# Where the two halves of a recurrence level stand on TensorE's queue, beside the attention blocks

## The chip, the cores and the metric

The kernel runs on one core of one Trainium2 chip. The metric is the device time of one execution in microseconds (us); of several runs the median is taken. In the rows, PE is TensorE, PEld its weight loads, DVE VectorE, ACT ScalarE, POOL GpSimd and SP SyncE.

## What is computed

One inference step of two hybrid decoder layers, for a prompt of 16 + 512 tokens and eight sample tokens. Each layer projects its input once and runs two mixers on the result: a sparse attention, in which an indexer picks the keys of each query, and a gated linear recurrence (HGRN2). Their outputs are gated, merged and projected, and a SwiGLU feed-forward follows. Of the recurrence the prompt's part matters here, computed in its exact chunk form:

```python
b = jnp.cumsum(logf.astype(jnp.float32), axis=1)
diff = b[:, :, None] - b[:, None, :]
decay = jnp.exp(jnp.where(causal[None, :, :, None, None], diff, -jnp.inf))
scores = jnp.einsum('bthk,bshk,btshk->bths', q, k, decay)
o = jnp.einsum('bths,bshv->bthv', scores, v) + jnp.einsum('bthk,bhkv->bthv', q * jnp.exp(b), S0)
```

and of the attention the softmax over the picked keys and its product with the values:

```python
s = jnp.where(valid[:, :, None, None, :], s, -jnp.inf)
p = jax.nn.softmax(s, axis=-1)
o = jnp.einsum('btngk,btknd->btngd', p, v_sel.astype(jnp.float32))
```

## The kernel before, in words

Each engine has its own instruction list, written out by hand; the lists meet only through semaphores. An engine works its list strictly in order, so a wait at its head holds up all that stands behind it. Most of a layer is one long run of weight units: 512 KB of weights are loaded, split by ACT and POOL into a high and a low part, and multiplied by PE in fp32. Between the input projection and the merge lies a stretch without weight units. In it 17 attention blocks (`BLK`, line 153; a block is one pair of heads by one tile of up to 128 queries) and the recurrence of the prompt are interleaved, over 20 steps of one loop (`STEPS`, line 144). The change lies in this stretch.

**An attention block** goes round three engines. PE multiplies queries and keys into `acc` (`qk`, line 1126, products at line 1143). DVE adds the mask and takes the row maximum (`att_scores`, line 2515, instruction at line 2528). ACT takes the exponential (`att_exps`, line 1739, at 1745), DVE the reciprocal of the sums (`att_recips`, line 2532, at 2536), ACT scales to probabilities (`att_probs`, line 1748, at 1754). PE turns the probabilities (`turn`, line 1147; transposes carry line 800), ACT copies them back to SBUF (`att_turned`, line 1756, at 1763), PE multiplies them with the values (`pv`, line 1162, products at line 1175) and ACT drains the result (`att_drain`, line 1646, at 1658). PE forms the query-key products two blocks ahead.

**The recurrence** splits the causal scores of a chunk of 128 tokens into a diagonal and seven levels, with blocks of 64, 32, 16, 8, 4, 2 and 1 tokens. For each level DVE forms differences of the summed log decays (`level_diff`), ACT takes their exponentials (`level_exp`, at line 1673), and DVE multiplies them with queries and keys (`level_product`, lines 2445 and 2447). PE multiplies the outcome with itself, for two heads at a time: the two halves of a level (`level`, line 1221, at 1227; eight fp32 products, which the trace shows as 16 records). DVE copies what the level's mask lets through into the score table `Asc` (`level_scores`, line 2411, at 2417). Four of the levels have a small product for the last 16 tokens besides (`level_tail`, line 1231, at 1238). Both halves of all levels use one PSUM tile, the whole of `work[1]`, and `rec_begin` (line 1181) makes a half wait until DVE has copied the half before:

```python
if n >= 1 and (rec_full(n) or rec_full(n - 1)):
    wait_rec_drained(pe, L, rec[n - 1])
```

**The order.** PE's loop works a block as: the steps of `PE_AHEAD`, the query-key products of the block after next, the turn of this block, the steps of `PE_AMID`, the value product of this block, the steps of `PE_BEHIND` (lines 1320 to 1335). DVE's loop (line 2540) works: the scores of the next block, `DVE_AHEAD`, the reciprocal of the next block, `DVE_BEHIND`; the copy of a level's first half is the last step of `DVE_BEHIND` in the level's block, that of the second half stands in `DVE_AHEAD` of the next block. ACT's loop (line 1773) works: probabilities, drain of the block before, exponentials of the next block, `ACT_AHEAD`, the turned probabilities, `ACT_BEHIND`. SP starts the load of the recurrence's sample states once the last level and tail are formed (line 614).

Of the kernel before, what the change touches and what calls it, by code (L numbers as in the profile page):

```python
# [76 lines left out]
def build(nc, t, out):  # L77
# [69 lines left out]
    for c in range(5):  # L147
# [3 lines left out]
    REC_ODD = [(RECS + 1) // 2, RECS // 2]  # L151
    TAILS = [7, 3, 4, 5, 6]
    BLK = [(0, 0), (0, 1), (0, 2), (0, 4), (0, 3)] + [(n2, j) for n2 in range(1, 4) for j in range(4)]
    PE_AHEAD = {1: [("diagonal", 0)], 2: [("diagonal", 1)], 4: [("level", 0, 0)], 6: [("level", 1, 0)],
                7: [("level", 2, 0)], 9: [("level", 3, 0), ("level_tail", 3)], 10: [("level", 4, 0), ("level_tail", 4)],
                12: [("level", 5, 0), ("level_tail", 5)], 13: [("level", 6, 0), ("level_tail", 6)]}
    PE_AMID = {3: [("v_turn", 3), ("v_turn", 4)], 4: [("level", 0, 1)],
               6: [("level", 1, 1)], 7: [("level", 2, 1)], 9: [("level", 3, 1)], 10: [("level", 4, 1)],
               12: [("level", 5, 1)], 13: [("level", 6, 1)], 14: [("decayed", 0)], 15: [("decayed", 1)],
               16: [("decayed", 2)], 17: [("decayed", 3)], 18: [("decayed", 4)]}  # L160
    PE_BEHIND = {3: [("level_tail", 7)], 14: [("rec_out", 0), ("state", 0), ("rank1", 0)], 15: [("rec_out", 1), ("state", 1), ("rank1", 1)],
                 16: [("rec_out", 2), ("state", 2), ("rank1", 2)], 17: [("rec_out", 3), ("state", 3)],
# [35 lines left out]
    with ctx:  # L198
# [62 lines left out]
        def place(name, shape, offset, dt=f32):  # L261

            n = 1
            for d in shape[1:]:
                n *= d
            n *= 1 if dt == u8 else 4
            assert offset + n <= size, (name, offset + n, size)
            return nc.alloc_sbuf_tensor_at(name, shape, dt, offset=base + offset)
# [56 lines left out]
        decayed = place("decayed", [P, 2, 512], 6 * TB + 5 * 2048)  # L325
# [469 lines left out]
        def _(pe):  # L795
# [18 lines left out]
            for L in range(DEPTH):  # L814
# [332 lines left out]
                def turn(block, s):  # L1147

                    n2, j = BLK[block]
                    ps = turn_tile_of(s)  # L1150
                    if L * BLOCKS + block:
                        pe.wait_ge(turn_drained[s], L * BLOCKS + block)
                        wait(pe, "pv_drained", L, BLOCKS, block)
                    wait(pe, "probs", L, 2 * BLOCKS, 2 * block + s + 1)
                    hold(pe)
                    for c in range(j + 1):
                        w = min(P, WIDTH[j] - c * P)
                        at = ps[0:w, c * P:c * P + P] if c < 4 else last_turn(s)
                        mm = transpose(at, scores_of(block, s, c * P, c * P + w))
                    mm.then_inc(turn_filled[s], 1)  # L1160
# [146 lines left out]
                def rec_steps(steps):  # L1307

                    for step in steps:
                        if isinstance(step, tuple):  # L1310
                            rec_step[step[0]](*step[1:])
                        else:
                            sample_turn(step)
# [6 lines left out]
                for block in range(STEPS):  # L1320
                    rec_steps(PE_AHEAD.get(block, ()))
                    if block + 2 < BLOCKS:
# [6 lines left out]
                    if block < BLOCKS:  # L1329
                        turn(block, 0)  # L1330
                        turn(block, 1)
                    rec_steps(PE_AMID.get(block, ()))
                    if block < BLOCKS:
# [1370 lines left out]
```

## Time and profile before

| | us |
|---|---|
| median of 3 runs | 2100.64 |
| lowest and highest | 2096.79, 2101.87 |
| the profiled execution | 2106.03 |
| its span, first to last instruction | 2104.1 |
| PE busy in the span | 1990.2 |

The profile is of one execution. Its page gives, per engine, the busy time, the chain of work that ended last, and the costliest groups of instructions; the trace behind it gives each instruction's start, length and, in brackets, how long its engine stood idle before it and what ended that.
### The profile page before, as it was taken

The numbers are of one execution on the slowest core, as the hardware profiler recorded it, in microseconds if no ns is written. First come the engines' busy times: TensorE is split into PE (matmuls) and PEld (weight loads), VectorE is DVE, ScalarE is ACT, GpSimd is POOL, SyncE is SP. The second block draws the span as 40 slices with busy tenths as digits, with TensorE's granted clock in tenths as the row PEclk, the third lists the DMA queues.
The fourth block names the chain that finished last, engine by engine and source line by source line (L and its number), as shares of the span: only waits on it lengthen the run. The fifth ranks groups of instructions, "written<-read, shape, count | busy, mean of one in ns | idle before, by whom it ended". The sixth has DMA issues, their size and how long they took to land.

```text
span 2104.1 us, 40077 instructions
## 1 busy us (share of the span) xinstructions
PE 1990.2 (95%) x15610; PEld 1889.6 (90%) x15610; DVE 1179.8 (56%) x2150; ACT 774.6 (37%) x1207; POOL 761.8 (36%) x418
## 2 busy tenths in 40 slices
PE   6999999888989999999999899998889999999998
PEld 6988899866889999999998889997678999999998
DVE  4477788676466442055346677986764664412531
ACT  4334222476234333222423342235652343322222
POOL 2633347200044434444455223661002444334342
PEclk9999999898899999999999999998998999999999
DMA  6332235202332332322241322442033323233322
GB/s 157 93 91 61 71 112 172 90 2 73 95 113 80 90 90 75 103 85 75 85 148 53 91 61 75 138 143 70 1 103 107 111 81 89 80 89 101 89 67 85
DMA packets 310126, 189.18 MB, mean 90 GB/s; under 512 B 15992, under 2 KB 295768, under 8 KB 308976
## 3 DMA queue, kind: packets, MB, share of 16 engines
q1 hardware_dynamic: 300368, 160.51, 26.9%
q0 software_dynamic: 4224, 16.78, 2.4%
q10 hardware_dynamic: 5408, 10.16, 1.4%
q8 instruction: 85, 1.39, 0.3%
q14 instruction: 41, 0.34, 0.1%
HBM read 167.47 MB, written 18.10 MB: 88 GB/s over the span
## 4 chain that ended last, share of the span: by engine, by line
PE 80%; DVE 7%; issue 5%; ACT 4%; POOL 3%; DMA 1%; POOLq 0%; SPq 0%; DVEq 0%; ACTq 0%
PE acc L839 64%; PE work L1227 3%; PE work L800 2%; POOL w_lo L685 2%; PE work L1175 1%; PE work L978 1%; POOL k_sel L751 1%; DVE std L1953 1%; PE acc L1143 1%; PE work L1262 1%; PE work L1081 1%; PE work L865 1%; PE work L1043 1%; DVE mix L2602 1%; ACT w_hi L1435 1%
## 5 line engine op out<-in xcount | busy, mean ns | idle before, releaser
L685 POOL TENSOR_TENSOR w_lo<-raw,w_hi 128x1024 fp32r<-128x1024 f32 (+3 forms) x290 | 623.8, 2152 | 1225.8 <-ACT w_hi L1435 1221.2
L839 PE MATMUL acc<-normed,w_hi 128*128 128x268 f32 x5696 | 958.5, 290 | 4.3 <-POOL w_lo L685 2.9
L839 PEld LDWEIGHTS acc<-normed,w_hi 128*128 128x128 f32 x5696 | 802.0, 190 | 27.3 <-issue 20.1
L1435 ACT ACTIVATE w_hi<-raw 128x1024 fp32r<-128x1024 f32 (+1 forms) x286 | 289.0, 1011 | 936.0 <-PE acc L839 936.0
L839 PE MATMUL acc<-normed,w_lo 128*128 128x268 f32 x2848 | 585.6, 287 | 0.0
L839 PEld LDWEIGHTS acc<-normed,w_lo 128*128 128x128 f32 x2848 | 446.3, 189 | 0.0
L839 PE MATMUL acc<-hidden,w_hi 128*128 128x268 f32 x1408 | 231.4, 286 | 0.0
L839 PEld LDWEIGHTS acc<-hidden,w_hi 128*128 128x128 f32 x1408 | 196.9, 188 | 0.0
L839 PE MATMUL acc<-hidden,w_lo 128*128 128x268 f32 x704 | 144.1, 286 | 0.0
L2639 DVE TENSOR_TENSOR hidden<-act_f,hidden 128x536 f32 x44 | 92.8, 2110 | 51.1 <-ACT hidden L1853 51.1
L2632 DVE TENSOR_TENSOR silu<-silu,rnorm 128x536 f32<-128x536 f32 x44 | 83.4, 1895 | 59.1 <-ACT silu L1850 59.1
L839 PEld LDWEIGHTS acc<-hidden,w_lo 128*128 128x128 f32 x704 | 109.7, 188 | 0.0
L2614 DVE TENSOR_TENSOR x<-acc,x 128x536 f32<-128x536 f32 x32 | 22.9, 717 | 127.5 <-PE acc L839 127.5
L839 PE MATMUL acc<-merged,w_hi 128*128 128x268 f32 x512 | 84.6, 287 | 4.8 <-issue 3.2
L2649 DVE TENSOR_TENSOR x<-acc,x 128x536 f32 x16 | 11.5, 716 | 125.6 <-PE acc L839 125.6
L2629 DVE TENSOR_TENSOR silu<-acc,rnorm 128x536 f32<-128x536 f32 x44 | 31.5, 717 | 84.7 <-PE acc L839 84.0
L1227 PE MATMUL work<-X 128*128 128x128 f32 x448 | 63.6, 301 | 16.2 <-issue 14.6
L1227 PEld LDWEIGHTS work<-X 128*128 128x128 f32 x448 | 59.1, 213 | 21.0 <-issue 20.9
L839 PEld LDWEIGHTS acc<-merged,w_hi 128*128 128x128 f32 x512 | 71.7, 188 | 5.6 <-issue 5.6
L2635 DVE TENSOR_TENSOR act_f<-acc,silu 128x536 f32<-128x536 f32 x44 | 31.5, 716 | 80.2 <-PE acc L839 80.0
L1467 ACT ACTIVATE relu<-work 128x256 f32<-128x256 f32 (+4 forms) x66 | 31.6, 503 | 85.9 <-PE work L978 68.1
L1929 DVE TENSOR_TENSOR proj_att<-acc,rnorm 128x536 f32<-128x536 f32 x26 | 18.4, 712 | 64.8 <-PE acc L839 59.0
(345 smaller groups left out, 2801.2 us busy)
## 6 DMA issues: line engine op xcount, KB each, us to landing
raw<-in_w_in_dram SPq DMA_DIRECT2D x90, 512.0 KB, 3.8
raw<-in_w_gu_dram SPq DMA_DIRECT2D x88, 512.0 KB, 3.8
raw<-in_w_down_dram SPq DMA_DIRECT2D x32, 384.0 KB, 3.3
raw<-in_w_down_dram SPq DMA_DIRECT2D x32, 320.0 KB, 3.0
gate_scratch<-gate_out ACTq DMA_DIRECT2D x32, 268.0 KB, 3.1
normed<-gate_scratch SPq DMA_DIRECT2D x4, 2144.0 KB, 9.8
raw<-in_w_o_dram SPq DMA_DIRECT2D x16, 512.0 KB, 3.9
raw<-in_w_pa_dram SPq DMA_DIRECT2D x16, 256.0 KB, 3.4
```

The costliest lines, as they stand in the source:

```text
L685: pool.tensor_tensor(w_lo[s][:, 0:kt, :], raw[slot][:, 0:kt, :], w_hi[s][:, 0:kt, :].bitcast(f32), ALU.subtract).then_inc(lo_done, 1)
L751: pool.indirect_dma_start(dst[:, i, :], None, rows, bass.IndirectOffsetOnAxis(row_idx[:, i:i + 1].bitcast(u32), 0))\
L800: return pe.transpose(dst, src, ident[0:k, 0:k])
L839: mm = pe.matmul(acc[o][:, half, 0:HT], w[s][:, k, :], mov[:, part, k0 + k, half * HT:(half + 1) * HT], start=start and n == 0, stop=stop ...
L1227: mm = pe.matmul(ps[:, m * P:(m + 1) * P], at[:, h, c * P:(c + 1) * P], at[:, h, c * P:(c + 1) * P], start=True, stop=True)
L1435: act.activation(w_hi[slot % 2][:, 0:kt, :], raw[slot][:, 0:kt, :], ACT.Copy).then_inc(hi_done, 1)
L1467: act.activation(dst, ps if src is None else src, func, **kw).then_inc(drained[slot_of(item)], 1)
L2614: TT(halves(x[:, k, :]), acc[i][:, :, 0:HT], halves(x[:, k, :]), ALU.add).then_inc(taken[i], 1)
L2629: TT(halves(silu[:, :]), acc[0][:, :, 0:HT], halves(rnorm[:, :]), ALU.mult).then_inc(taken[0], 1)
L2632: TT(silu[:, :], silu[:, :], rnorm[:, :], ALU.mult).then_inc(S["up_scaled"], 1)
L2635: TT(halves(act_f[:, :]), acc[1][:, :, 0:HT], halves(silu[:, :]), ALU.mult).then_inc(taken[1], 1)
L2639: TT(hidden[:, 1, ds(g, 1), :].rearrange("p a t -> p (a t)"), act_f[:, :], hidden[:, 0, ds(g, 1), :].rearrange("p a t -> p (a t)").bitcast ...
```

## The change

Two of PE's step tables are rewritten, nothing else. In the blocks 4, 6, 7, 9, 10, 12 and 13 the first half of a level, and with it the tail where there is one, moves from `PE_AHEAD` to `PE_AMID`, ahead of the second half, which was there before. So both halves now come behind the turn of the block's probabilities and ahead of its value product. The lists of DVE, ACT, POOL and SP are as before.

```diff
-    PE_AHEAD = {1: [("diagonal", 0)], 2: [("diagonal", 1)], 4: [("level", 0, 0)], 6: [("level", 1, 0)],
-                7: [("level", 2, 0)], 9: [("level", 3, 0), ("level_tail", 3)], 10: [("level", 4, 0), ("level_tail", 4)],
-                12: [("level", 5, 0), ("level_tail", 5)], 13: [("level", 6, 0), ("level_tail", 6)]}
-    PE_AMID = {3: [("v_turn", 3), ("v_turn", 4)], 4: [("level", 0, 1)],
-               6: [("level", 1, 1)], 7: [("level", 2, 1)], 9: [("level", 3, 1)], 10: [("level", 4, 1)],
-               12: [("level", 5, 1)], 13: [("level", 6, 1)], 14: [("decayed", 0)], 15: [("decayed", 1)],
+    PE_AHEAD = {1: [("diagonal", 0)], 2: [("diagonal", 1)]}
+    PE_AMID = {3: [("v_turn", 3), ("v_turn", 4)], 4: [("level", 0, 0), ("level", 0, 1)],
+               6: [("level", 1, 0), ("level", 1, 1)], 7: [("level", 2, 0), ("level", 2, 1)],
+               9: [("level", 3, 0), ("level_tail", 3), ("level", 3, 1)],
+               10: [("level", 4, 0), ("level_tail", 4), ("level", 4, 1)],
+               12: [("level", 5, 0), ("level_tail", 5), ("level", 5, 1)],
+               13: [("level", 6, 0), ("level_tail", 6), ("level", 6, 1)], 14: [("decayed", 0)], 15: [("decayed", 1)],
                16: [("decayed", 2)], 17: [("decayed", 3)], 18: [("decayed", 4)]}
```

## Rows read from the trace of the kernel before

**Rows 1.** The page: the chain that ended last, shares of the span by engine.
```profile
PE 80%; DVE 7%; issue 5%; ACT 4%; POOL 3%; DMA 1%; POOLq 0%; SPq 0%; DVEq 0%; ACTq 0%
```

**Rows 2.** Busy times by stretch (PE, PEld, DVE, ACT, POOL), clock, DMA: levels, layer 0.
```profile
444.00:512.00 68.00, 53.95 (x442) 43.34 (x440) 48.82 (x91) 46.82 (x122) 0.00 (x0) 0.94 0.00 1
```

**Rows 3.** PE in order of time (start, length, instruction, idle before), block 4.
```profile
441.99 3.56 PE L1227 MATMUL work<-X 128*128 128x128 f32 x16
...
447.12 1.95 PE L1227 MATMUL work<-X 128*128 128x128 f32 x16
```

**Rows 4.** DVE's masked copies: one in order of time, then all of line 2417.
```profile
445.69 0.73 DVE L2417 COPY_PREDICATED Asc<-level_mask,work 128x512 f32<-128x512 uint8 x1 [0.95 <-PE work L1227]
...
L2417 DVE COPY_PREDICATED Asc<-level_mask,work x28: 693/722/1310, 445.7 to 1544.1; 128x512 f32<-128x512 uint8 x28
```

**Rows 5.** PE in order of time, blocks 5 to 7 of layer 0.
```profile
452.78 0.44 PE L1175 MATMUL work<-pT,tok 128*64 128x128 f32 x4 [1.46 <-ACT pT L1763]
454.00 2.02 PE L1227 MATMUL work<-X 128*128 128x128 f32 x16 [0.78 <-DVE X L2447]
455.95 0.69 PE L1143 MATMUL acc<-k_dup,proj_att 64*128 64x512 f32 x1
...
457.01 0.66 PE L800 MATMUL work<-cst,raw 128*128 128x128 f32 x4
459.05 2.02 PE L1227 MATMUL work<-X 128*128 128x128 f32 x16 [1.38 <-issue]
461.00 0.66 PE L1175 MATMUL work<-pT,tok 128*64 128x128 f32 x8
462.04 2.02 PE L1227 MATMUL work<-X 128*128 128x128 f32 x16 [0.38 <-issue]
...
465.46 2.02 PE L1227 MATMUL work<-X 128*128 128x128 f32 x16 [0.17 <-issue]
```

**Rows 6.** DVE in order of time, block 6 of layer 0.
```profile
454.72 0.08 DVE L2528 DVE_READ_ACCUMULATOR2_ANT row_st<- 128x1 f32 x1
...
457.09 1.22 DVE L2447 TENSOR_TENSOR X<-X,K 128x1024 f32<-128x1024 f32 x1
458.23 0.72 DVE L2417 COPY_PREDICATED Asc<-level_mask,work 128x512 f32<-128x512 uint8 x1
```

**Rows 7.** PE in order of time, later blocks of layer 0; last, level 1 of layer 1.
```profile
477.26 2.02 PE L1227 MATMUL work<-X 128*128 128x128 f32 x16 [1.26 <-issue]
...
480.23 2.02 PE L1227 MATMUL work<-X 128*128 128x128 f32 x16 [0.57 <-issue]
482.18 0.36 PE L1238 MATMUL acc<-X 128*16 128x16 f32 x8
...
490.24 1.55 PE L1175 MATMUL work<-pT,tok 128*64 128x128 f32 x12 [2.37 <-ACT pT L1763]
...
498.36 2.02 PE L1227 MATMUL work<-X 128*128 128x128 f32 x16 [1.82 <-issue]
...
507.27 3.58 PE L1227 MATMUL work<-X 128*128 128x128 f32 x16 [1.80 <-issue]
...
1493.70 2.02 PE L1227 MATMUL work<-X 128*128 128x128 f32 x16 [1.38 <-issue]
```

**Rows 8.** DVE in order of time, block 12 of layer 0.
```profile
494.56 0.17 DVE L2536 RECIPROCAL row_st<-row_st 128x2 f32<-128x2 f32 x1 [3.30 <-ACT E L1745]
```

**Rows 9.** Busy times by stretch as in rows 2, near blocks 5 and 11.
```profile
452.00:454.00 2.00, 0.44 (x5) 0.26 (x5) 2.00 (x3) 2.00 (x6) 0.00 (x0) 1.00 0.00 0
...
490.00:492.00 2.00, 1.76 (x13) 1.46 (x14) 1.27 (x5) 2.00 (x6) 0.00 (x0) 0.51 0.00 0
492.00:494.00 2.00, 2.00 (x13) 2.00 (x14) 0.00 (x0) 2.00 (x7) 0.00 (x0) 0.63 0.03 8
...
1524.00:1526.00 2.00, 1.09 (x11) 1.12 (x12) 1.93 (x6) 2.00 (x5) 0.00 (x0) 0.57 0.00 0
...
1530.00:1532.00 2.00, 2.00 (x19) 1.42 (x19) 2.00 (x3) 0.37 (x2) 0.00 (x0) 0.72 0.00 0
```

## The prediction

> **What bounds the kernel now.** I read the page's chain first: 80% of the chain that ended last is work of TensorE (PE) [rows 1]. So whatever makes PE stand still longer makes the kernel longer, unless a gap that is there already takes it up. Next come the busy times by stretch: in the stretch with the attention blocks and the recurrence levels PE is busy only 53.95 of 68 us. There no engine is full (VectorE, DVE, 48.82; ScalarE, ACT, 46.82) [rows 2]: the time is set by a chain that goes round PE, DVE and ACT. The change lies in this stretch alone, once in each of the two layers, so I then read the order in time of PE and DVE there, block by block. Layer 1 has the same order and, where PE's clock is the same, the same gaps (1.38 ahead of the second half of level 1 in both [rows 5, 7]).
>
> **The change, part by part.** No instruction is added or taken away; no DMA is issued in what moves, and SP, POOL and ACT keep their order. On PE's queue, in blocks 4, 6, 7, 9, 10, 12 and 13, the first half of a level (16 matmul records, 2.02 us at full clock [rows 5]) and in four of them a tail of the level go behind the next query-key products and the turn of the probabilities. Both halves write the same PSUM tile, so the second half waits for DVE's masked copy of the first. Today the query-key products and the turn stand between the two and cover that copy; after the change nothing does, but for the tail. What queues behind the waiting matmul is the value product of the block; ACT's drain of it, and behind that drain ACT's exponentials of two blocks on, wait for it.
>
> The price of the bare round trip: the first half of level 0 ends at 441.99 + 3.56 = 445.55 [rows 3], its copy starts at 445.69 and takes 0.73 [rows 4], and another copy ends at 458.23 + 0.72 = 458.95 [rows 6] with PE's second half at 459.05 [rows 5]: 0.14 + 0.73 + 0.10 = 0.97 us. Copies of the last two levels take up to 1.31 [rows 4], so 1.55. This is paid in full only where the first half's end is what comes last. I walk the seven levels of layer 0 with today's durations:
>
> Level 0 (block 4). Today the second half starts at 447.12 with no gap [rows 3], the cover is whole. After: +0.97. The query-key products and the turn just change places with the half.
>
> Block 5 passes this on: its value product waits for ACT, 1.46 idle [rows 5], and ACT comes from the drain of block 4.
>
> Level 1 (block 6). The products that the first half waits for, and DVE's scores of block 7 behind them, come 0.97 late. Those scores end today at 454.72 + 0.08 = 454.80 [rows 6]; after, at 455.77, and PE's next query-key products start 0.10 later at 455.87 instead of 455.95 [rows 5]. So the delay is gone for a moment, because the first half no longer stands ahead of them. They and the turn take 1.72 (455.95 to 457.67 [rows 5]), hardly overlapped, and the first half ends near 455.87 + 1.72 + 2.02 - 0.07 = 459.54; DVE's second product, today 457.09 + 1.22 [rows 6], ends at 459.28 and is no longer last. With the round trip the second half starts at 460.51; today 459.05. The delay is now 1.46, so this level adds 0.49.
>
> Level 2 (block 7). From the value product at 461.00 to the second half at 465.46 PE has gaps of 0.38 and 0.17 [rows 5]; the first goes, the second becomes 0.97, less what overlap is left: 4.46 - 0.55 + 0.97 = 4.88, so +0.42.
>
> Level 3 (block 9). Today's 1.26 idle ahead of the second half [rows 7] is DVE finishing its products ahead of the copy. DVE arrives as late as everything else and is again last: +0, and the first half fills the gap without a gain. Bounds: 0 to the bare round trip less the tail that now stands in it (0.36 [rows 7]), 0.6.
>
> Level 4 (block 10). 0.57 idle ahead of the first half goes [rows 7]; 0.97 less the tail's 0.3 comes: +0.1.
>
> Levels 5 and 6 (blocks 12 and 13). DVE has waited 3.30 us for ACT's exponentials [rows 8] and then does products and copy; PE's 1.82 and 1.80 idle [rows 7] are that wait. It shifts as a whole: +0 each, bounds 0 to 1.55 - 0.36 = 1.2.
>
> Sum: 0.97 + 0.49 + 0.42 + 0 + 0.1 + 0 + 0 = 2.0 us a layer, 4.0 in both.
>
> **The clock** is the term that the trace of before doesn't show directly. After the turn of block 5 PE has today 1.46 idle, 0.44 of value product, 0.78 idle [rows 5]: 2.24 idle, and the clock granted there was 1.00 [rows 9]. After the change it has 1.46, 0.44, and then nothing until 455.87, where the product ended at 454.19: 1.68, so 3.14 idle with 0.44 of work in it. The nearest row on the other side is the gap ahead of the value product of block 11: after 2.37 us without a matmul [rows 7] PE came back at the lower level of its clock (1.2 instead of 2.4 GHz), 0.51 granted in 490 to 492 and 0.63 in 492 to 494 [rows 9]. That is (0.49 + 0.37) x 2 = 1.7 us of PE time lost. In layer 1 the same gap cost (0.43 + 0.50 + 0.50 + 0.28) x 2 = 3.4 [rows 9], the two rows left out both showing 0.50. So the new hole is longer than the one that went unpunished and longer than the one that was punished: I take a fall, at the price of layer 0, 1.7, and keep 0 and 3.4 as bounds. PE is last in block 6 after the change, so what the clock takes is all on the path. The Trainium skill (TensorE: Matmul & The Clock Gate, section "A second HAM failure mode: psum-queue depth-cycling") tells of a kernel that cycled through its PSUM tiles and whose clock went up and down at the short idle spells between groups, so speaks against this change; the trace agrees as far as 0.51 behind the 2.37 us gap goes. Without that page the term stays as it is.
>
> Per layer 2.0 + 1.7 = 3.7, together +7.4 us. The profiled execution took 2106.03 us (span 2104.1), 5.4 above the median of the runs shown (2100.64); its own time would become 2113.4. Nothing in the sum depends on that offset, so I put it on the median: **2108.0 us**.
>
> **The rivals.** (A) The clock holds in block 6, and only the walk counts: +4.0, 2104.6. For it: 2.24 us of idle in the same place cost nothing. Against it: 3.14 is beyond both the 2.24 that kept the clock and the 2.37 that lost it.
>
> (B) Every copy laid bare is paid in full. The Trainium skill (Perfetto Trace Analysis, section "Optimizing Tensor Performance") says that independent matmul groups should rotate through PSUM banks so that the evacuation of one overlaps the matmuls of the next; here both halves of a level share a tile, and the change takes away the other work that stood in for such a rotation. Worked out from rows: 5 x 0.97 + 2 x 1.55 - 4 x 0.36 = 6.5 a layer, 13.0 in both, 2113.6. Against it: in blocks 6, 9, 12 and 13 the idle ahead of the second half (1.38, 1.26, 1.82, 1.80 [rows 5, 7]) is already longer than the round trip, so part of it finds room.
>
> (C) Not slower: PE alone decides. The gaps that PE has today ahead of the halves, 0.78 + 1.38 + 0.38 + 0.17 + 1.26 + 0.57 + 1.82 + 1.80 = 8.2 us a layer [rows 5, 7], would be filled by the moved halves and the earlier query-key products, and 6.5 of round trips put in their place: -1.7 a layer, 2097.3. It decides if DVE stands ready when a first half ends, that is, if the copy isn't queued behind products. Against it: the copy at 458.23 shows no idle ahead of it [rows 6], DVE came straight from the product at 457.09; and DVE's scores of the block after next stand behind the copy on DVE's queue, so the earlier query-key products buy nothing there.
>
> **How the numbers follow.** The forecast, walk plus fall of the clock, 0.52; (A) 0.27; (B) 0.12; (C) 0.09. 0.3%, about what a measurement of this kernel can tell from no change, is 6.3 us. The forecast and (B) lie beyond it: slower 0.64. (A) and the nearer half of (C) lie within: same 0.32. Faster by more than 0.3% would take (C) and one of today's low stretches of the clock going away besides: 0.04. The range: at the low end the walk's 4.0 less one low stretch of today that doesn't come back (1.7), less the scatter of the runs shown (2096.79 to 2101.87, some 1.5 from the median): 2101.5. At the high end two layers of 2.0 + 3.4 with one late level at its bound of 1.2: 13.2, and 1.2 of scatter: 2115.
>
> **What would show it.** In the trace of after, PE should sit idle about 0.97 us ahead of the second halves of levels 0, 1 and 2, with DVE's copy as what it waits for, and the copies of these levels should now wait for PE; if the copies show no idle, (C) gains. The first half of level 1 should take over 3 us instead of 2.02, with 0.5 to 0.8 granted around it, in both layers; if it takes 2.02 the clock term was wrong and (A) stands. The idle ahead of the second halves of levels 3, 5 and 6 should stay about what a product on DVE leaves (1 to 1.5 us after the tail); if it is added on top, (B) stands. The time from the end of the value product of block 3 to that of block 13 should grow by 2.0 + 1.7 us in each layer, and nothing outside it should change but by the clock's phase. That phase is what could make the prediction wrong beyond these cases: a low stretch that moves off or onto a dense piece shifts the time by 1.7 to 3.4 us without any part in the change.

## The result and the profile after

| | before | after |
|---|---|---|
| median of four runs, side by side (us) | 2099.58 | 2120.97 |
| lowest and highest | 2096.79, 2101.87 | 2118.89, 2121.76 |
| ratio, 95% interval | | 1.0092 [1.0074, 1.011] |
| the profiled execution | 2106.03 | 2120.83 |
| its span | 2104.1 | 2118.8 |

The change makes the kernel 21 us slower, far beyond the forecast of 2108.0 and above the range's end of 2115. All lines of the kernel after stand one higher than before (1227 is now 1228). The shares of the chain that ended last are as in [rows 1], but for ACT's 3%:

```profile
PE 80%; DVE 7%; issue 5%; ACT 3%; POOL 3%; DMA 1%; POOLq 0%; SPq 0%; DVEq 0%; ACTq 0%
```

So the page doesn't show the loss; the order in time does. PE after, blocks 4 to 6 of layer 0 (start, length, instruction, idle before); it answers [rows 3, 5]:

```profile
446.29 2.07 PE L1228 MATMUL work<-X 128*128 128x128 f32 x16
...
449.33 2.02 PE L1228 MATMUL work<-X 128*128 128x128 f32 x16 [0.97 <-issue]
...
455.06 0.44 PE L1176 MATMUL work<-pT,tok 128*64 128x128 f32 x4 [1.46 <-ACT pT L1764]
457.19 1.19 PE L1144 MATMUL acc<-k_dup,proj_att 64*128 64x512 f32 x1 [1.70 <-DVE row_st L2529]
...
459.20 1.11 PE L801 MATMUL work<-cst,raw 128*128 128x128 f32 x4
460.11 3.62 PE L1228 MATMUL work<-X 128*128 128x128 f32 x16
464.69 2.02 PE L1228 MATMUL work<-X 128*128 128x128 f32 x16 [0.97 <-issue]
```

The two halves of levels 0 and 1 follow each other with the bare round trip of 0.97 between them (0.96 at level 2). Behind the hole (1.46 idle, 0.44 of work, 1.70 idle) PE comes back slow: the first query-key product of block 8 takes 1.19 instead of 0.69, the turn 1.11 instead of 0.66, the first half of level 1 takes 3.62 instead of 2.02 [rows 5]. DVE's masked copies of the first halves now wait for PE; that of level 1 came straight behind a product in [rows 6]. After, levels 0, 1 and 5 of layer 0, DVE in order of time:

```profile
448.51 0.72 DVE L2418 COPY_PREDICATED Asc<-level_mask,work 128x512 f32<-128x512 uint8 x1 [2.38 <-PE work L1228]
...
463.88 0.72 DVE L2418 COPY_PREDICATED Asc<-level_mask,work 128x512 f32<-128x512 uint8 x1 [3.28 <-PE work L1228]
...
505.08 1.29 DVE L2418 COPY_PREDICATED Asc<-level_mask,work 128x512 f32<-128x512 uint8 x1 [2.09 <-PE work L1228]
```

PE after, levels 3 to 6 of layer 0, against [rows 7]:

```profile
483.12 2.02 PE L1228 MATMUL work<-X 128*128 128x128 f32 x16 [1.20 <-issue]
...
489.90 2.02 PE L1228 MATMUL work<-X 128*128 128x128 f32 x16 [0.66 <-issue]
...
496.17 0.88 PE L1176 MATMUL work<-pT,tok 128*64 128x128 f32 x12 [2.40 <-ACT pT L1764]
...
499.80 1.94 PE L801 MATMUL work<-cst,raw 128*128 128x128 f32 x8 [1.70 <-ACT proj_att L1659]
501.53 3.40 PE L1228 MATMUL work<-X 128*128 128x128 f32 x16
...
506.47 2.02 PE L1228 MATMUL work<-X 128*128 128x128 f32 x16 [1.25 <-issue]
...
515.37 3.38 PE L1228 MATMUL work<-X 128*128 128x128 f32 x16 [2.56 <-issue]
```

Levels 3 and 4 keep their pace. In block 12 the turn now waits 1.70 for ACT's drain of block 11, which the first half of level 5 used to cover, and behind that wait the turn and the first half run slowly, 1.94 and 3.40.

The table puts the traces of seven kernels side by side, by the starts of the levels' second halves in PE's order in time. Each entry is the time in us from the second half of the level before to that of the level named, layer 0 / layer 1; "behind" is the time from the second half of level 6 to the end of the last state product of block 18. A second half that is itself slow shows in the row of the level behind it. The last five columns belong to the experiments. Each column is one execution.

| level | before | after | before, 2nd trace | undo_6 | undo_12 | undo_6_12 | after_fill |
|---|---|---|---|---|---|---|---|
| 1 | 11.92 / 11.93 | 15.36 / 13.95 | 11.93 / 11.93 | 12.06 / 12.05 | 15.36 / 13.76 | 12.05 / 12.06 | 12.33 / 12.34 |
| 2 | 6.41 / 6.41 | 6.63 / 6.63 | 6.42 / 6.42 | 6.57 / 6.58 | 6.72 / 6.63 | 6.58 / 6.57 | 6.72 / 6.63 |
| 3 and 4 | 18.58 / 18.57 | 18.57 / 18.56 | 18.57 / 18.56 | 18.57 / 18.57 | 18.57 / 18.56 | 18.57 / 18.57 | 18.57 / 18.56 |
| 5 | 14.33 / 14.34 | 16.58 / 15.85 | 14.37 / 14.34 | 16.60 / 16.55 | 14.39 / 14.40 | 14.42 / 14.39 | 14.40 / 14.44 |
| 6 | 8.91 / 8.91 | 8.90 / 8.90 | 8.92 / 8.91 | 8.90 / 8.90 | 10.49 / 8.90 | 10.49 / 10.49 | 8.90 / 8.90 |
| behind | 47.92 / 39.56 | 42.24 / 46.23 | 41.48 / 39.57 | 42.25 / 42.24 | 48.00 / 47.92 | 48.02 / 48.04 | 42.60 / 42.69 |
| the profiled execution | 2106.03 | 2120.83 | 2099.77 | 2112.05 | 2127.01 | 2119.09 | 2108.93 |

From the first to the second trace of before nothing but "behind" in layer 0 differs by more than 0.1 us within the table, and it makes 6.4 of the 6.5 us between their spans. The profiled execution that the prediction was built on took 4.2 us longer than the longest of the runs beside it (2101.87). Three executions in a slower state of the chip (before at 2234.64 and 2247.46, before_fill at 2793.97) are in no ratio of this document. Set against the second trace (span 2097.6), after loses 21.2 us of span: 1.7 up to the second half of level 0 (from the first diagonal half: 25.22 to 26.58 and 25.73 to 26.06), 3.43 + 2.02 at level 1, 0.4 at level 2, 2.21 + 1.51 at level 5, 0.76 + 6.66 behind the levels, and some 2.5 elsewhere, of it 1.95 between the two layers' parts. The medians, 21.4 apart, agree with this pair; the first trace of before is only 14.7 of span from after.

### The profile page after: what moved, and what is told of

It is laid out like the page before. It is cut to its first block, busy times and chain, and to the rows that moved or that the text cites. A ratio compares the mean times of both kernels' runs of the same rounds, so it can differ in the third digit from the quotient of the medians.

```text
span 2118.8 us, 40077 instructions
## 1 busy us (share of the span) xinstructions
PE 1997.1 (94%) x15610; PEld 1895.7 (89%) x15610; DVE 1180.1 (56%) x2150; ACT 774.5 (37%) x1207; POOL 761.5 (36%) x418
## 4 chain that ended last, share of the span: by engine, by line
PE 80%; DVE 7%; issue 5%; ACT 3%; POOL 3%; DMA 1%; POOLq 0%; SPq 0%; DVEq 0%; ACTq 0%
PE acc L840 63%; PE work L1228 3%; PE work L801 2%; POOL w_lo L686 2%; PE work L979 1%; PE work L1176 1%; POOL k_sel L752 1%; PE acc L1144 1%; DVE std L1954 1%; PE work L1263 1%; PE work L1082 1%; PE work L866 1%; PE work L1044 1%; DVE mix L2603 1%; ACT w_hi L1436 1%
## 5 line engine op out<-in xcount | busy, mean ns | idle before, releaser
L2650 DVE TENSOR_TENSOR x<-acc,x 128x536 f32 x16 | 11.5, 717 | 125.6 <-PE acc L840 125.6
```

## The experiments

All edits stand in PE's queue alone. "Behind" is the last row of the table's parts.

**A second trace of before** (no edit).

> The kernel before once more, for a second trace of it. Theory (what follows the levels is a matter of where in a stretch the clock falls, and differs from run to run): the time is 2099.6 us within 3, and the trace shows the same intervals up to the value product of block 13 within 0.5 us, but other stretches at the lower clock behind it than the profiled run of 2106.0 had (it had 0.50 at 524 to 528 us and 0.60 to 0.73 beside it, 44.3 us from that product to the first product of the output units in layer 0 against 37.5 in layer 1). Rival (the low clock behind the levels belongs to the program): the same 44.3 and 37.5 us again.

Measured: 2102.59 us, ratio 1.0001 [0.9989, 1.0012]. The theory holds for layer 0, the rival for layer 1. The blocks behind the levels in the first trace and then in the second, both layers (stretch; length, busy PE, PEld, DVE, ACT, POOL; granted clock; DMA):

```profile
507.27:555.19 47.92, 44.84 (x263) 37.38 (x263) 23.77 (x62) 17.26 (x41) 0.00 (x0) 0.78 0.40 123
1541.94:1581.51 39.57, 36.49 (x263) 29.21 (x263) 23.77 (x62) 17.27 (x41) 0.00 (x0) 0.97 0.48 149
```
```profile
507.31:548.79 41.48, 38.49 (x263) 31.11 (x263) 23.77 (x62) 17.23 (x41) 0.00 (x0) 0.91 0.47 142
1535.56:1575.12 39.56, 36.47 (x263) 29.21 (x263) 23.77 (x62) 17.24 (x41) 0.00 (x0) 0.97 0.49 150
```

The same 263 matmul records take 36.5 to 44.8 us of PE time, and what moves with it is the granted clock, 0.97 to 0.78. DVE's and ACT's work is the same to 0.1 us.

**Undoing block 6, block 12, and both.** The edit of undo_6_12; the others make one half of it:

```diff
-    PE_AHEAD = {1: [("diagonal", 0)], 2: [("diagonal", 1)]}
+    PE_AHEAD = {1: [("diagonal", 0)], 2: [("diagonal", 1)],
+                6: [("level", 1, 0)], 12: [("level", 5, 0), ("level_tail", 5)]}
     # PE_AMID, the other entries cut:
-               6: [("level", 1, 0), ("level", 1, 1)], 7: [("level", 2, 0), ("level", 2, 1)],
+               6: [("level", 1, 1)], 7: [("level", 2, 0), ("level", 2, 1)],
-               12: [("level", 5, 0), ("level_tail", 5), ("level", 5, 1)],
+               12: [("level", 5, 1)],
```

> The change, but with block 6 as before: the first half of level 1 ahead of the scores of block 8 and of the turn. Theory (each level's loss is its own, as the two traces have it: level 1 costs 3.43 us in layer 0 and 2.04 in layer 1): 5.5 us less than the changed kernel, 2121.0 - 5.5 = 2115.5 us, and the first half of level 1 at 2.0 us again (3.62 and 2.23 in the changed kernel). Rival (what was lost in block 6 only moves everything behind it, and the loss of some 10 us behind the levels comes from one of the moved levels): if it hangs on block 6 the time falls by 5.5 + 10 to 2105.5; if nothing hangs on it, because the lost time returns as waiting in block 7 or 9, 2121.

> The change, but with block 12 as before: the first half of level 5 and the tail of level 5 ahead of the scores of block 14 and of the turn. Theory (the loss of level 5 is its own: 2.24 us in layer 0, 1.52 in layer 1): 3.8 us less than the changed kernel, 2117.2 us; the gap of 1.70 us ahead of the turn of block 12, which ends with ScalarE's copy of block 11's value product, is gone, and the first half of level 5 takes 2.0 us (3.40 in the changed kernel). Rival (the low clock behind the levels hangs on block 12): 2121.0 - 3.8 - 10 = 2107 us. Rival (ScalarE, busy without a gap there, sets the pace with either order): 2121.

> The change in blocks 4, 7, 9, 10 and 13 alone; blocks 6 and 12 as before. Theory (losses add up by level): 2121.0 - 5.5 - 3.8 = 2111.7 us if the 10 us behind the levels stay, of which levels 0 and 2 hold 2.3 (1.85 and 0.43 in both layers). Prediction's bare walk without its clock term: levels 0, 2 and 4 cost 0.97 + 0.42 + 0.1 in each layer, 2099.6 + 3.0 = 2102.6 us, which holds if the rest of the loss hung on blocks 6 and 12. Rival: anything over 2112 says that levels 0, 2, 3, 4 or 6 carry a loss that the two traces did not show as theirs.

Measured beside a before of 2103.37: undo_6 2112.19, ratio 1.0047 [1.0031, 1.0062]; undo_12 2120.59, 1.008 [1.0062, 1.0098]; undo_6_12 2118.9, 1.0071 [1.0055, 1.0087]. In the levels each undoing gives back what the theory said (table: level 1 falls from 15.36 / 13.95 to 12.06 / 12.05, level 5 from 16.58 / 15.85 to 14.39 / 14.40). In the whole time it is otherwise. Each set beside its own before, the change loses 21.4 us by the medians, undo_6 8.8, undo_12 17.2 and undo_6_12 15.5, where the theory's sums come to 15.9, 17.6 and 12.1. So undo_6 gives back more than the 5.5 of level 1 (12.6 by the medians, some 9.5 by the ratios): in its trace level 1 is 5.2 us shorter than in after, and the blocks behind are 4.0. The time of undo_12 agrees with the theory, but its interval overlaps the change's as well, so the time can't tell whether anything was won. Undoing both gives, by the medians, less than undoing block 6 alone, with overlapping intervals. The traces of undo_12 (its longest execution, 2127.01 of down to 2117.48) and undo_6_12 show where a gain goes: to level 6 (10.49 in three of their four layers) and to the blocks behind (48.0 in all four). In undo_12, PE at the two halves of level 5, of which the second stood at 2.02 in [rows 7]; and the blocks behind:

```profile
499.44 3.17 PE L1229 MATMUL work<-X 128*128 128x128 f32 x16
...
506.78 3.58 PE L1229 MATMUL work<-X 128*128 128x128 f32 x16 [1.87 <-issue]
```
```profile
517.27:565.26 47.99, 44.90 (x263) 37.41 (x263) 23.77 (x62) 16.04 (x38) 0.00 (x0) 0.78 0.40 123
```

The first half, back ahead of the scores, is still slow (3.17, in layer 1 2.87, where 2.0 was expected) but costs nothing there; in layer 0 the low clock is found on the second half too, and in both layers in the blocks behind. The same is to be seen in undo_6, PE at level 1 of layer 0:

```profile
454.72 3.21 PE L1229 MATMUL work<-X 128*128 128x128 f32 x16 [0.79 <-DVE X L2449]
...
459.83 1.97 PE L1229 MATMUL work<-X 128*128 128x128 f32 x16
```

The first half is slow here too, 3.21 us, yet level 1 takes 12.06, only 0.13 above before: ahead of the scores it has slack. Behind the turn it has hardly any.

**Holes filled, in the change and in before.** Products of constants, whose results nobody uses, in PE's idle time:

```diff
+    def fill(n):
+        for _ in range(n):
+            pe.matmul(acc[1][:, 1, 256:384], C("ident"), C("ident"), start=True, stop=True)
     # after_fill:  PE_AMID 5: fill 4;  PE_AHEAD 6: fill 6;  PE_AMID 11: fill 8
     # before_fill: PE_AMID 11: fill 8;  PE_AMID 12 and 13: fill 6 ahead of the level
```

> The change, with products of 128x128 whose results nobody uses in TensorE's holes: four behind the turn of block 5 (1.46 us idle there), six ahead of the scores of block 8 (1.70 idle), eight behind the turn of block 11 (2.40 idle). Nothing that the reference needs is moved. Theory (the loss at levels 1 and 5 beyond the walk is the clock alone): the first half of level 1 takes 2.02 us in both layers (3.62 and 2.23 in the changed kernel) and level 1 costs 11.93 + 0.5 from second half to second half (15.36 and 13.95); the turn of block 12 takes 1.1 (1.94) and level 5 costs 14.33 again (16.58 and 15.85), though the wait for ScalarE's drain stays; in sum 2.9 + 1.5 + 2.2 + 1.5 = 8.1 us of the levels' loss go. Rival (level 5's loss is the queue on ScalarE ahead of the drain of block 11, which the first half used to hide): level 5 stays at 15.6 or more. The whole time can go either way with the pattern of blocks 14 to 18: 2121 - 8.1 = 2113 if that stays.

> The kernel before, with products of 128x128 whose results nobody uses in the holes from block 11 on: eight behind the turn of block 11 (2.37 us idle), six ahead of the second halves of levels 5 and 6 (1.82 and 1.80 idle). Theory (the low stretches there follow on those holes): no granted clock below 1.00 from block 11 to the second half of level 6, its first record of 3.5 us back at 2.02; what that gives is 0 to 1.5 us a layer in the levels, since level 5 had slack for its low stretch, and blocks 14 to 18 take 39.6 us in both layers if they start at the full clock: 2103.4 - 2 to - 9. Rival (the clock falls behind the rank-one products and the single columns of blocks 14 to 16 whatever went before): blocks 14 to 18 stay between 41 and 48 us, and the time within 3 us of 2103.4 or above it.

Measured: after_fill 2108.93, ratio to before 1.0028 [1.0017, 1.0039], where the change had 1.0092. PE at levels 1 and 5 of layer 0, and the busy times by stretch around them:

```profile
459.94 1.95 PE L1228 MATMUL work<-X 128*128 128x128 f32 x16
462.87 2.02 PE L1228 MATMUL work<-X 128*128 128x128 f32 x16 [0.97 <-issue]
...
498.06 1.06 PE L801 MATMUL work<-cst,raw 128*128 128x128 f32 x8 [1.81 <-ACT proj_att L1664]
498.96 1.95 PE L1228 MATMUL work<-X 128*128 128x128 f32 x16
...
502.56 2.02 PE L1228 MATMUL work<-X 128*128 128x128 f32 x16 [1.35 <-issue]
```
```profile
454.00:466.00 12.00, 10.29 (x83) 8.07 (x80) 10.30 (x19) 8.58 (x24) 0.00 (x0) 1.00 0.00 1
490.00:505.00 15.00, 10.99 (x109) 9.48 (x109) 9.46 (x19) 12.96 (x36) 0.00 (x0) 1.00 0.01 1
```

The same stretches in after:

```profile
455.00:465.00 10.00, 7.28 (x31) 5.33 (x32) 6.72 (x12) 6.02 (x15) 0.00 (x0) 0.66 0.00 0
496.00:506.00 10.00, 7.13 (x48) 6.23 (x48) 4.59 (x9) 9.52 (x29) 0.00 (x0) 0.66 0.01 2
```

With the clock at 1.00 the first halves are back at 1.95, level 1 at 12.33 / 12.34 and level 5 at 14.40 / 14.44: 3.03 + 1.61 + 2.18 + 1.41 = 8.2 us gone, as forecast (8.1). The turn of block 12 still waits 1.81 for ACT, so the rival, ACT's queue, falls: that wait costs nothing when the clock holds. The whole gains more than the 8.2 (by the ratios 1.0092 - 1.0028 = 0.64%, 13 us); in the traces another 3.2 comes from behind the levels, 88.5 to 85.3 in both layers together.

before_fill: 2105.58, ratio 1.0009 [0.9998, 1.002], no gain. The theory failed here: block 11 was at full clock, but the low clock came later, level 6 took 10.21 us in both layers, and the blocks behind took 40.9. The low clock in block 11 of before had cost nothing (level 5 takes 14.38 without it), so there was nothing to win. The products ahead of the last two levels aren't what lengthened level 6, for the experiments below show it without them. In before's order the first half of level 5 ran at full clock (2.05) in before_fill, before_pause4, before_early and before_block0, and level 6 took 10.2 to 11.5 in all eight layers; it was slow (2.87 to 3.79) in both traces of before, before_pause8 and before_tail, and level 6 took 8.9 in all eight.

**A pause in before.** Four or eight such products in block 4 behind the turn, where the change puts its first late copy:

```diff
-    PE_AMID = {..., 4: [("level", 0, 1)],
+    PE_AMID = {..., 4: [("fill", 4), ("level", 0, 1)],      # or 8
```

> The kernel before, with no level moved, and four products of 128x128 (about 1.0 us, results unused) put on TensorE's queue in block 4 behind the turn, where the change puts its first late copy of 0.97 us. Theory (much of the change's loss is not in the moved work: blocks 14 to 18, which the change leaves alone, took between 39.6 and 48.0 us in the traces so far, with 2.6 to 20.7 us of it at the lower clock, and which of these it is follows from the moment at which the levels end): the 1.0 us moves everything behind it by as much as undo_6_12 was moved, so level 6 and blocks 14 to 18 fall into the long pattern (48 us) too, and the time is near undo_6_12's: 2103.4 + 2.0 + up to 2 x 8 = 2113 to 2119 us. Rival (each piece of work costs its own length): 2103.4 + 2.0 = 2105.4 us.

> As before_pause4 with eight products, about 2.0 us. Theory (the moment at which the levels end picks the pattern of what follows): the time isn't that of before_pause4 plus 2.0, but another pattern; with the 39.6 to 42.2 us one behind both levels it is 2103.4 + 4.0 - 0 to 3 = 2104 to 2108 us, so possibly less than with half the added work. Rival (each piece costs its own length): 2103.4 + 4.0 = 2107.4, and 2.0 above before_pause4 in any case.

Measured beside a before of 2101.85: 2107.07, ratio 1.0022 [1.0013, 1.0031], and 2107.45, 1.003 [1.0021, 1.0039]. The first refutes the theory as I had put it: 1.0 us at the same place didn't bring undo_6_12's 48 us; the blocks behind took 41.41 / 41.32. Yet the cost, 5.2 by the medians, is above the rival's 2.0 as well. In the profiled execution, its longest (2110.00), the second half of level 5 fell to the lower clock in both layers, and level 6, counted from it, took 10.51 / 10.52, 3.2 more in both together than in before. PE, layer 0:

```profile
503.12 3.24 PE L1227 MATMUL work<-X 128*128 128x128 f32 x16 [3.33 <-issue]
```

The second is 5.6 above its before, or 4.4 to 8.2 by the interval: above the rival's 4.0, and at the upper end of the theory's 0.6 to 4.6 or beyond it. The two intervals overlap, and whether it is 2.0 above the first can't be told. What follows: with a delay of 1 us far ahead the low clock falls on other instructions, at level 6 as the theory had it, but the blocks behind don't follow.

**Extra products behind the levels, in both kernels.**

```diff
 # rank1(h), h < 3, ahead of the product; chunk_out(c), c in (1, 2), likewise with ps
+    for _ in range(4):
+        pe.matmul(rank_tile(h, 0)[:, 0:P], C("ident"), C("ident"), start=True, stop=True)
```

> The kernel before, with four extra products of 128x128 (about 1.0 us) ahead of each rank-one product of blocks 14 to 16 and ahead of the first products of the outputs of chunks 1 and 2 (behind the single-column products of blocks 15 and 16); they write where the next instruction writes over them. Theory (the low stretches of blocks 14 to 18 come where these little products follow one another, and the extra products hold the clock there): from the second half of level 6 to the last state product 39.6 - 1.2 + 5 = 43.4 us in both layers, with less than 4 us of it at the lower clock; the time 2102 + 3 to 8 us. Rival (the clock falls in these blocks whatever PE does there): low stretches of 7 to 20 us stay, and the part takes 46 to 53 us.

> The change with the same extra products as before_tail. Theory (blocks 14 to 18 are the same work in both kernels, and only the moment at which they begin differs): with the clock held there, this kernel and before_tail differ by what the levels alone lose, 11.3 us in the traces (1.7 at level 0, 5.5 at level 1, 0.4 at level 2, 3.7 at level 5) and up to 2 us ahead of them, not by 18 to 21. Rival (blocks 14 to 18 lose time because of the moved halves themselves, the queues behind them being late): the difference from before_tail stays at 18 or more, and the part from level 6 to the last state product is 3 us longer here than there.

Measured beside a before of 2102.16: 2116.92, ratio 1.0072 [1.0058, 1.0085], and 2121.55, 1.0088 [1.0074, 1.0102]. The blocks behind the levels, before_tail and then after_tail:

```profile
507.96:552.90 44.94, 41.85 (x303) 34.62 (x303) 23.76 (x62) 17.25 (x41) 0.00 (x0) 0.95 0.41 127
1542.22:1587.16 44.94, 41.86 (x303) 34.60 (x303) 23.77 (x62) 17.26 (x41) 0.00 (x0) 0.95 0.41 127
```
```profile
513.63:558.19 44.56, 41.47 (x303) 34.22 (x303) 23.77 (x62) 16.05 (x38) 0.00 (x0) 0.96 0.41 127
1551.29:1595.85 44.56, 41.48 (x303) 34.21 (x303) 23.76 (x62) 16.04 (x38) 0.00 (x0) 0.96 0.41 127
```

With more work in it the part takes the same time in all four places, 44.6 to 44.9, at 0.95 to 0.96; without it 39.6 to 48.0. The 43.4 us expected were not reached, and before_tail is 14.8 above its before, where 3 to 8 were expected. In the change the same products cost nothing that can be told: the ratio is 1.0088, that of the change 1.0092. The moved halves don't make these blocks longer: they take 0.38 less in after_tail. The rival falls. The two kernels differ by 4.6 us by their medians and by 9.9 in the spans of their profiles (2110.6 and 2120.5); both are less than the 11.3 expected, and the medians by much. The profiled execution of before_tail was its fastest, 2112.67 of up to 2120.61, and where its other executions lost more no trace shows.

**A fill ahead of the levels in before.** before_early has fourteen products ahead of the scores of block 2 and eight behind the turn of block 11; before_block0 the fourteen alone:

```diff
-    PE_AHEAD = {1: [("diagonal", 0)],
+    PE_AHEAD = {0: [("fill", 14)], 1: [("diagonal", 0)],
```

> The kernel before, with products whose results nobody uses in two holes: fourteen (3.5 us) ahead of the scores of block 2, where TensorE stands idle for 4.0 us waiting for VectorE's scores, and eight behind the turn of block 11 (2.37 us idle). Theory (a hole brings the lower clock to what follows it): no low stretch behind the hole of block 0 (13.65 us of it in the second trace of before, with the first diagonal half at 3.76 us instead of 2.02) and none behind block 11; the levels begin 1 to 4 us earlier in each layer, and the time is 2 to 8 us less than before's 2102, with blocks 14 to 18 between 39.6 and 42 us; if those fall into the pattern of 48 us it is the same as before. Rival (what is late there is DVE and ACT, not PE): nothing changes ahead of the levels, and the time is 2102 within 4 us, as before_fill's was.

> The kernel before with only the first fill of before_early: fourteen products whose results nobody uses ahead of the scores of block 2, where TensorE stands idle for 4.0 us; the hole of block 11 stays as it is. Theory (a low stretch costs only where TensorE is what comes last: behind block 11 it falls on the first half of level 5, which has slack, and in before_early, where it was taken away there, it came at level 6, 10.4 and 11.5 us instead of 8.9): the levels begin 1.5 to 3 us earlier in each layer as in before_early, level 5 takes 14.3 with its low stretch, level 6 8.9 us, and the time is 2102 - 3 to 6 = 2096 to 2099 us, less than before. Rival (what is gained ahead of the levels only shifts the moment at which blocks 14 to 18 begin, and they take it back): 2100 to 2104 us, with 42 to 48 us in those blocks in at least one layer.

Measured: before_early 2100.29, ratio 0.9993 [0.9983, 1.0003], undecided; its profiled execution, one of its longer ones (2105.86), has 10.41 / 11.53 at level 6 and 42.8 behind. before_block0 2100.2 beside 2104.09, ratio 0.9982 [0.9969, 0.9995]: faster than before, and so than both kernels, by 4 us. The second trace of before and then before_block0, blocks 0 to 2, block 4:

```profile
412.00:426.00 14.00, 9.33 (x46) 5.72 (x50) 8.91 (x36) 8.22 (x24) 0.00 (x0) 0.51 0.51 150
440.00:446.00 6.00, 6.00 (x72) 5.13 (x70) 3.27 (x5) 2.51 (x7) 0.00 (x0) 0.73 0.01 3
```
```profile
412.00:426.00 14.00, 11.05 (x82) 8.21 (x90) 9.52 (x36) 8.39 (x25) 0.26 (x1) 0.88 0.52 151
440.00:446.00 6.00, 6.00 (x78) 5.38 (x76) 4.06 (x9) 3.23 (x10) 0.00 (x0) 1.00 0.00 0
```

From the first diagonal half to the second half of level 0 it needs 23.45 / 23.39 instead of 25.22 / 25.73. The theory's levels didn't come as told: block 11 was at full clock although its hole stood unfilled, and level 6 took 10.51 in both layers, where 8.9 was expected, which gives back 3.2 of the 4.1 won. The rival's sign, 42 us or more behind the levels in at least one layer, isn't there either (41.1 and 40.2). Beside its own before the gain of 3.9 is what the theory expected (3 to 6), though not by the way it named. Against the second trace of before, the shortest of that run's 11 executions, its span is only 0.4 us shorter (2097.2); the 4 us are the medians'.

## Why the prediction was wrong

Of the 21.2 us between the second trace of before and after, the forecast had 7.4. The 13.8 that it lacked are 3.7 at level 5, 7.4 in the blocks behind the levels, 2.5 elsewhere outside them and 1.1 at level 1, less 0.9 by which levels 0, 2 and 4 came out cheaper. So one step was wrong, level 5 at "+0", and two terms of the clock were sized too small, above all the one outside the levels. The time from the value product of block 3 to that of block 13, forecast to grow by 3.7 a layer, grew by 6.5 and 4.7.

*The walk* was right. Round trip: 0.97 forecast, 0.96 to 0.98 ahead of the second halves of levels 0, 1 and 2, with DVE's copies of levels 0 and 1 waiting for PE. Where the clock is held, in after_fill, level 1 costs 0.40 (0.49 forecast), level 2 0.21 to 0.30 (0.42), levels 3, 4 and 6 nothing, level 5 0.07 to 0.10; in layer 1 of undo_6_12 the way from the first diagonal half to the second half of level 0 takes 26.64 for 25.72, 0.9 (0.97), with the same part of it lost to the clock in both, 5.1. Some 1.7 us a layer, where 2.0 was forecast. Rival (C) is out, and (B) as well: the idle ahead of the second halves of levels 3 and 5 is 1.20 and 1.25, not 0.97 more than it was. Ahead of that of level 6 it is 2.56, above the 1 to 1.5 forecast, but 0.53 and 1.80 stood ahead of its two halves before, and the level keeps its 8.9.

*The clock in block 6* was the right mechanism, mis-sized. The hole was read right (1.46 + 0.44 + 1.70 for 3.14 idle with 0.44 of work), and the clock fell. Taken was 1.7 a layer; it cost 3.03 and 1.61, both within the bounds of 0 to 3.4. The sign given, a first half of over 3 us in both layers, held in layer 0 alone (3.62); in layer 1 it took 2.23, and the low clock lay on the products ahead of it. Rival (A) is out.

*Levels 5 and 6, "+0 each"* is the step that failed. The walk counted today's wait for ACT's exponentials as something that shifts as a whole, and set PE's part beside it at full-clock durations. But [rows 9] show 0.51 and 0.63 right there, and the prediction used them to price block 6 and not block 12. In before the slow work (the first half of level 5) stood ahead of the turn, where PE waits for DVE later on anyway. Moved behind the turn, it is what comes last: 2.25 and 1.51 us, all but 0.1 of it clock, as after_fill shows. The bound of 1.2 held the copy and the tail, and nothing for the clock.

*"Nothing outside it should change but by the clock's phase"* was right as a sentence, and its size wrong. It was set at 1.7 to 3.4 and left out of the range, whose high end has 1.2 of scatter beside the walk and block 6. The blocks behind the levels alone take between 39.6 and 48.0 us a layer for the same instructions. Between the second trace of before and after they make 7.4 of 21.2 us; between the first trace and after 1.0. In the traces of undo_12 and undo_6_12 they, with level 6, took back all that the levels had won. That this is the clock, and neither the queues nor SP's later load of the sample states, is shown twice: by their equal length with extra work in both kernels, and by the granted clock itself. In the 24 layers of the twelve traces without that work their length times the clock granted in them is 37.3 to 38.3 us, while the length goes from 39.6 to 48.0. Of the 2.5 elsewhere, the 1.95 between the two layers' parts go with the clock as well: the time lost to it there (length times one less the granted clock) is 14.4 us in after and 11.8 in both traces of before.

The Trainium skill (TensorE: Matmul & The Clock Gate, section "Part 1: The HAM clock gate") says of the ramp at a kernel's start that the same kernel shows a different count of slow matmuls from run to run, and that for modelling the ramp's penalty is under 1% of a typical span. Here the low stretches lie inside the kernel, and the two traces of before, 6.5 us apart, show that they too differ between executions. Taken for them, the 1% would have made the term small; the clock's part at levels 1 and 5 is 8.2 us and that behind the levels 7.4, together 0.74% of 2102.6: under 1%, and still most of the effect.

*What stays open:* why one pattern of low clock and not another is met behind the levels, and why all four runs of after lie so close together (2118.89 to 2121.76). before_pause4 speaks against the moment alone as the cause, and so do the two traces of before, as the last section shows. Nor was it tried whether two PSUM tiles for the two halves would take back the walk's 1.7 us; as the kernel stands, the attention blocks hold its other PSUM tensors.

## What to carry to other kernels

When an instruction is moved, walk it with the durations that the trace shows at that place, the clock included: slow work costs nothing where the engine waits later on anyway, and most or all of its length where it is last. Independent work between two users of one tile is cover for their round trip and for a low clock at once, so its loss can be paid twice, as at level 1 here. A small change shifts everything behind it; an unchanged stretch whose length depends on the granted clock can give or take more than the change itself, so read it in several traces before its scatter goes into a range.

## What the runs showed of the hardware

The clock falls not only behind idle holes, and not always at the same place. Blocks 14 to 16 of layer 0 in the first trace of before, then the last stretch once more in the second:

```profile
517.40:520.70 3.30, 3.30 (x16) 1.74 (x14) 2.57 (x11) 1.68 (x5) 0.00 (x0) 1.00 1.04 405
520.80:531.00 10.20, 10.04 (x52) 9.74 (x52) 1.82 (x4) 2.71 (x7) 0.00 (x0) 0.50 0.48 147
519.00:531.00 12.00, 11.76 (x64) 10.82 (x62) 3.40 (x10) 3.52 (x8) 0.00 (x0) 0.57 0.57 185
```
```profile
519.00:531.00 12.00, 11.41 (x95) 9.09 (x94) 7.68 (x23) 5.10 (x11) 0.00 (x0) 1.00 0.57 190
```

In the first trace PE is busy without a gap for 3.3 us, with rank-one products and transposes, and is then granted 0.50 for 10.2 us, in which it is busy 10.04. In the second trace the rank-one products begin at 517.46 instead of 517.49, behind a second half of level 6 that is as slow (3.52 and 3.58), and the clock stays at 1.00. So neither idle time, nor the instructions, nor the moment in the span tells by itself where the clock falls.

Filling a hole went with a higher clock behind it (0.51 to 0.88 in blocks 0 to 2, 0.66 to 1.00 at levels 1 and 5), but the fall can come later instead, as at level 6 in before_fill, before_early and before_block0.
